# Hybrid diffusion backbone step: the modulation product in four units per tile of the attention with half sums, and the output projection's first weights split in quarters

## The chip, the cores and the metric

The kernel runs on one core of one Trainium2 chip. The metric is the device time of one execution in microseconds: 1143.93 us is the median of three executions of the kernel before, which lay between 1142.75 and 1150.54 us.

## What is computed

One step of a backbone of two layers on 640 tokens of width 1024 (512 latent ones and 128 of context), all in float32. Cut to what matters here, a layer is

```
mod = silu(c) @ w_ada + b_ada                  # 1024 x 6144: shift1, scale1, gate1, shift2, scale2, gate2
h = rms_norm(x, norm1) * (1 + scale1) + shift1
q, k, v, ... = split(h @ w_in)                 # 8 query heads, 2 key heads, width 64
attn = softmax(q k^T) v                        # context rows read context keys, latent rows all 640
merged = concat(rms_norm(attn), rms_norm(sgu), rms_norm(conv))
x = x + gate1 * (merged @ w_out)
h2 = rms_norm(x, norm2) * (1 + scale2) + shift2
x = x + gate2 * hierarchical_moe(h2)           # 16 experts, 2 for each token
```

`mod` is needed for two vectors only (latent `c`, context `c_ctx`). Its first third is due before `h`; the other two thirds (gate1 on) are due after the attention.

## The kernel before, in words

Each engine has its own instruction list, written out by hand, and runs it in order; semaphores join the lists. TensorE (PE) multiplies, ScalarE (ACT) and VectorE (DVE) move results and do the softmax, GpSimd (POOL) does small statistics, the convolution and some transfers, SyncE (SP) issues the loads of the weights.

**Weights.** They come through `raw`, a ring of `RAWS` = 4 buffers of 1 MB, in the fixed order `STREAM`: in a layer eight units of `w_in`, then 16 units of `w_ada` (numbers 8 to 23), then four units of `w_out` (w 8 to 11). SP loads a unit when the one four places ahead has been used (`unit_used`, L355 and L362). A `w` unit is used by splitting it for a product of float32 accuracy: ACT copies it, rounded, to `wH` (`split_hi`, L651, 128x2048), and DVE writes the rest `raw - wH` to `wL` (`split_lo`, L997). An `ada` unit is used by PE straight from `raw` (`ada_mm`, L1407): 4 products of 512 columns in program text, for 128 of the 1024 input rows and 2048 of the columns of `mod`. Eight of them sum up one piece in PSUM bank 7. DVE adds the bias (`piece_add`, L970), and POOL writes the piece to DRAM (`piece_out`) and later loads it back as rows for all partitions.

**Attention.** Five tiles of 128 query rows, first the context tile, whose rows read 128 keys, then four latent ones with 640 keys. Each tile has 8 heads; a head of a tile is a step u, from 0 to 39. Four more values of u finish the last ones. In the step u
- PE makes the scores of u (L1514, L1515), transposes the probabilities of u-2 (L1525), and in an even step multiplies those of a pair of heads with the values (L1540). In an odd step it transposes a pair's result (L1530). In the first two steps of a tile it transposes queries of the next tile (`q_round`, L1493), into bank 7 too, so that a piece has to be read before;
- DVE takes the row maximum of u (L1122), copies transposed probabilities of an even head (L1130), and in an odd step divides a pair (`pair_out`, L1092, L1093). At the third step of a tile it makes the low part of queries (`q_lo`, L1021); at steps 16, 24, 32 and 40 it scales a finished tile (L1099);
- ACT copies transposed probabilities of an odd head (L780), takes the exponential of u (L787), copies a pair's result (L741), and squares finished tiles (L746).

The maximum of u waits for the scores of u; the exponential waits for the maximum; the scores of u+2 wait for the exponential of u, since there are two buffers.

**What stands at which step** is set by two tables. `ADA_AT` gives the number of `ada` units of PE at the end of each step: 0, 0, 1, 1, 1, 1, 2, 2 in the first tile and 0, 0, 2, 2, 1, 1, 1, 1 in the third. `PIECE_AT` follows from it: DVE sums up at the steps 7 and 23. `W_AT` places the splits of w 8 and w 9 on ACT and DVE at the steps 33 and 37, in the last tile. Units w 10 and w 11 are split after the attention.

After the last step PE transposes the merged rows (`merged_chunk`, L1567) and starts the output projection with w 8.

Of the kernel before, what the change touches and what calls it, by code (L numbers as in the profile page):

```python
# [19 lines left out]
NT = 5  # L20
NLT = 4
# [9 lines left out]
N = 512  # L31
# [22 lines left out]
for _l in range(DEPTH):  # L54
# [9 lines left out]
    "ada_read": 24, "piece_done": 3, "piece_out": 2 * 64, "bias_in": 3 * 64,  # L64
    "norm2_row": 16, "a2_row": 2, "params_loaded": 15 * 16, "taps_loaded": 32, "tabs": 6, "modc_psum": 1, "a1_ready": 1,
    "ss1": NT, "rstd1": NT, "xr_ready": NT, "hT_psum": KD, "h_full": 2 * KD, "h_hi": KD, "h_lo": KD,
    "w_hi": 12, "w_lo": 12, "w_used": 6, "proj": 4 * NT, "proj_read": 4 * NT, "zpn_zero": 2,
# [17 lines left out]
def build(nc, I, O):  # L85
    with ExitStack() as ctx:
# [169 lines left out]
        def unit_used(eng, i):  # L256

            kind, l, n = STREAM[i]
            if kind == "ada":
                eng.wait_ge(sem("ada_read"), at("ada_read", l, n + 1))  # L260
            else:
                eng.wait_ge(sem("w_lo"), at("w_lo", l, n + 1))
# [183 lines left out]
        def _(pl):  # L446
# [49 lines left out]
            for l in range(DEPTH):  # L496
# [34 lines left out]

                piece_out(l, 1)
                bias_in(l, 2)
                rest_stats(0)
                attn_stats(0)
# [81 lines left out]
        def _(act):  # L617
# [27 lines left out]
            for l in range(DEPTH):  # L645
                def split_hi(i):
# [4 lines left out]
                    act.activation(wH[:, i % HLS, :], raw[:, POS["w", l, i] % RAWS, :], ACT.Copy).then_inc(sem("w_hi"), 1)  # L651

# [117 lines left out]
                for u in range(NT * NH + 4):  # L770
# [18 lines left out]
                    if u in W_AT:  # L789
                        split_hi(W_AT[u])  # L790
# [150 lines left out]
        def _(dve):  # L941
# [29 lines left out]

            def modc_out(l):
# [21 lines left out]
            for l in range(DEPTH):  # L994
                def split_lo(i):
                    dve.wait_ge(sem("w_hi"), at("w_hi", l, i + 1))
# [118 lines left out]
                for u in range(NT * NH + 4):  # L1115
# [17 lines left out]
                    if u in W_AT:  # L1133
                        split_lo(W_AT[u])
# [9 lines left out]
                    if u in PIECE_AT:  # L1144
                        piece_add(l, 1 + PIECE_AT.index(u))
# [238 lines left out]
        def _(pe):  # L1384
# [37 lines left out]
            for l in range(DEPTH):  # L1422
# [26 lines left out]
                for i in range(8):  # L1449
                    nb, half = divmod(i, 2)  # L1450
                    for k in range(4):
# [3 lines left out]
                        if k == 0:  # L1455
                            pe.wait_ge(sem("w_lo"), at("w_lo", l, i + 1))
# [45 lines left out]
                for u in range(NT * NH + 4):  # L1502
# [90 lines left out]
                for kt in range(KD):  # L1593
                    i, k = 8 + kt // 4, kt % 4
                    pe.wait_ge(sem("mT_lo"), at("mT_lo", l, 2 * kt + 2))
                    if k == 0:
                        pe.wait_ge(sem("w_lo"), at("w_lo", l, i + 1))
# [10 lines left out]
                for t in range(NT):  # L1608
                    if t >= 2:
                        pe.wait_ge(sem("oproj"), at("oproj", l, NT + t - 1))  # L1610
                    for kt in range(KD):
                        i, k = 10 + kt // 4, kt % 4
                        if t == 0 and k == 0:
                            pe.wait_ge(sem("w_lo"), at("w_lo", l, i + 1))
# [146 lines left out]
```

## Time and profile before

| | |
|---|---|
| median of three executions | 1143.93 us |
| the profiled execution's own time | 1141.14 us |
| span of its instructions | 1139.3 us |
| mean granted clock of TensorE | 0.915 |
| busy: PE, DVE, ACT, POOL | 943.4, 673.7, 590.3, 264.5 us |
| PE: idle just before `ada_mm` (L1407) | 33.7 us, of them 33.2 for loads of `w_ada` |

The span lies 1.8 us below the time of its execution. Times of the trace count from the span's start. A busy figure is a mean over stages with different limits, so what matters is which wait ends last in the stage that is changed: the attention, some 116 us of layer 0 and 114 us of layer 1. A row of the timeline gives start, duration, engine, line, operation, and in brackets the idle time before it with what ended it.

### The profile page before, as it was taken

The numbers are of one execution on the slowest core, as the hardware profiler recorded it, in microseconds if no ns is written. First come the engines' busy times: TensorE is split into PE (matmuls) and PEld (weight loads), VectorE is DVE, ScalarE is ACT, GpSimd is POOL, SyncE is SP. The second block draws the span as 40 slices with busy tenths as digits, with TensorE's granted clock in tenths as the row PEclk, the third lists the DMA queues.
The fourth block names the chain that finished last, engine by engine and source line by source line (L and its number), as shares of the span: only waits on it lengthen the run. The fifth ranks groups of instructions, "written<-read, shape, count | busy, mean of one in ns | idle before, by whom it ended". The sixth has DMA issues, their size and how long they took to land.

```text
span 1139.3 us, 14992 instructions
## 1 busy us (share of the span) xinstructions
PE 943.4 (83%) x5232; PEld 737.7 (65%) x5232; DVE 673.7 (59%) x929; ACT 590.3 (52%) x901; POOL 264.5 (23%) x306
## 2 busy tenths in 40 slices
PE   3799988996999499999319999799789949999920
PEld 0488864775778278887218888377568837888710
DVE  0349223565264689989372941365635758998946
ACT  1662233665232288888275332366623408888832
POOL 3024016011041112221250410620202312222133
PEclk9999997998898699999759999899989959999975
DMA  9955227342153989999771240636223358999853
GB/s 323 273 211 209 74 60 305 156 168 86 56 212 112 369 313 399 413 409 366 191 276 47 74 148 10 241 144 267 97 72 130 107 201 303 398 421 417 345 186 128
DMA packets 85951, 248.36 MB, mean 218 GB/s; under 512 B 25644, under 2 KB 30252, under 8 KB 75656
## 3 DMA queue, kind: packets, MB, share of 16 engines
q1 hardware_dynamic: 72760, 209.54, 49.0%
q0 software_dynamic: 11696, 32.86, 8.4%
q10 hardware_dynamic: 1440, 5.24, 1.1%
q8 instruction: 33, 0.54, 0.2%
q14 instruction: 22, 0.18, 0.1%
HBM read 221.07 MB, written 30.21 MB: 221 GB/s over the span
## 4 chain that ended last, share of the span: by engine, by line
PE 65%; DMA 14%; DVE 8%; ACT 7%; issue 4%; POOL 1%; SPq 0%; ACTq 0%; POOLq 0%; DVEq 0%
PE ps L1390 12%; PE ps L1392 11%; PE ps L1391 11%; DMA pool<-in_moe_w 7%; DMA raw<-in_w_ada 4%; PE ps L1540 3%; PE ps L1407 3%; PE ps L1397 3%; PE ps L1399 3%; PE ps L1398 3%; PE ps L1525 3%; DVE wL L1196 2%; ACT wH L841 2%; PE ps L1514 2%; PE ps L1656 2%
## 5 line engine op out<-in xcount | busy, mean ns | idle before, releaser
L1390 PE MATMUL ps<-wH,actH 128*128 128x512 f32 x608 | 247.3, 407 | 7.5 <-DVE actL L1325 5.9
L1392 PE MATMUL ps<-wH,actL 128*128 128x512 f32 x608 | 240.7, 396 | 0.0
L1391 PE MATMUL ps<-wL,actH 128*128 128x512 f32 x608 | 239.8, 394 | 0.0
L1196 DVE TENSOR_TENSOR wL<-raw,wH 128x2048 fp32r<-128x2048 f32 x64 | 146.2, 2285 | 12.2 <-ACT wH L841 12.1
L841 ACT ACTIVATE wH<-raw 128x2048 fp32r<-128x2048 f32 x64 | 122.4, 1912 | 30.7 <-DMA raw<-in_moe_w 27.7
L1390 PEld LDWEIGHTS ps<-wH,actH 128*128 128x128 f32 x608 | 116.5, 192 | 32.9 <-issue 8.5
L1392 PEld LDWEIGHTS ps<-wH,actL 128*128 128x128 f32 x608 | 115.9, 191 | 25.7
L1391 PEld LDWEIGHTS ps<-wL,actH 128*128 128x128 f32 x608 | 116.5, 192 | 22.6
L1397 PE MATMUL ps<-wH,actH 128*128 128x512 f32 x256 | 105.4, 412 | 4.2 <-DVE wL L1196 2.8
L1399 PE MATMUL ps<-wH,actL 128*128 128x512 f32 x256 | 102.2, 399 | 0.0
L1398 PE MATMUL ps<-wL,actH 128*128 128x512 f32 x256 | 101.6, 397 | 0.0
L581 POOL DMA_INDIRECT pool<-h2s,idxc x28 | 52.3, 1867 | 195.7 <-PE ps L1656 156.6
L1122 DVE TENSOR_REDUCE nmax<-ps 128x1 f32<-128x640 f32 (+1 forms) x80 | 57.3, 716 | 63.8 <-PE ps L1515 62.3
L1407 PE MATMUL ps<-raw,cpad 128*32 128x512 f32 x384 | 64.0, 760 | 33.7 <-DMA raw<-in_w_ada 33.2
L1196 DVE TENSOR_TENSOR wL<-pool,wH 128x2048 fp32r<-128x2048 f32 x32 | 73.2, 2287 | 15.8 <-ACT wH L841 15.8
L787 ACT ACTIVATE pool<-ps,nmax 128x640 f32<-128x640 f32 (+1 forms) x80 | 56.5, 706 | 46.4 <-DVE nmax L1122 42.8
L997 DVE TENSOR_TENSOR wL<-raw,wH 128x2048 fp32r<-128x2048 f32 x24 | 54.7, 2291 | 29.0 <-ACT wH L651 28.8
L1525 PE MATMUL ps<-ident,pool 128*128 128x128 f32 x336 | 54.5, 289 | 16.7 <-DVE pool L1130 14.2
L651 ACT ACTIVATE wH<-raw 128x2048 fp32r<-128x2048 f32 x24 | 45.9, 1930 | 38.4 <-PE ps L1392 38.4
L841 ACT ACTIVATE wH<-pool 128x2048 fp32r<-128x2048 f32 x32 | 61.2, 1912 | 5.0 <-DMA pool<-in_moe_w 5.0
L1397 PEld LDWEIGHTS ps<-wH,actH 128*128 128x128 f32 x256 | 49.2, 192 | 15.9 <-DVE wL L1196 3.8
L877 ACT ACTIVATE actH<-ps 128x512 fp32r<-128x512 f32 x64 | 38.3, 598 | 39.3 <-PE ps L1656 36.9
(228 smaller groups left out, 1579.6 us busy)
## 6 DMA issues: line engine op xcount, KB each, us to landing
raw<-in_w_ada SPq DMA_DIRECT2D x48, 1024.0 KB, 7.3
raw<-in_moe_w SPq DMA_DIRECT2D x96, 512.0 KB, 8.4
raw<-in_w_in SPq DMA_DIRECT2D x16, 1024.0 KB, 9.1
raw<-in_moe_w SPq DMA_DIRECT2D x16, 1024.0 KB, 13.1
pool<-in_moe_w SPq DMA_DIRECT2D x32, 512.0 KB, 8.1
pool<-in_moe_w SPq DMA_DIRECT2D x16, 1024.0 KB, 12.9
ys<-pool SPq DMA_DIRECT2D x32, 512.0 KB, 12.1
raw<-in_w_out SPq DMA_DIRECT2D x8, 1024.0 KB, 7.7
```

Of the source, the lines that this page charges most:

```text
L787: act.activation(prob[:, u % 2, 0:keys], flat[:, 2 * N * (u % 2):2 * N * (u % 2) + keys], ACT.Exp, bias=nmax[:, u % 2:u % 2 + 1], accum_ou ...
L841: act.activation(wH[:, i if place is None else place, :], mraw[parity][i], ACT.Copy).then_inc(sem(f"m_hi{i}"), 1)
L1122: dve.tensor_reduce(nmax[:, u % 2:u % 2 + 1], flat[:, 2 * N * (u % 2):2 * N * (u % 2) + keys], X, ALU.max, negate=True).then_inc(sem("nmax ...
L1196: dve.tensor_tensor(wL[:, w, :], mraw[parity][i], f32(wH[:, w, :]), ALU.subtract).then_inc(sem(f"m_lo{i}"), 1)
L1390: pe.matmul(out, aH, wH[:, slot_, cols_], start=first, stop=False)
L1391: pe.matmul(out, aH, wL[:, slot_, cols_], start=False, stop=False)
L1392: return pe.matmul(out, aL, wH[:, slot_, cols_], start=False, stop=last)
L1397: pe.matmul(out, aH, hi, start=first, stop=False)
L1398: pe.matmul(out, aH, lo, start=False, stop=False)
L1399: return pe.matmul(out, aL, hi, start=False, stop=last)
L1407: m = pe.matmul(ps[32 * j:32 * j + 32, ada_bank(l, q), :], c32, raw[:, POS["ada", l, n] % RAWS, j * N:(j + 1) * N], start=(kt == 0), stop= ...
L1525: m = pe.transpose(ps[:, 4 + c // 4, (c % 4) * P:(c % 4) * P + P], prob[:, w % 2, c * P:(c + 1) * P], ident[:, :])
```

## The change

- `ADA_AT` is now 0, 0, 1, 1, 1, 1, 0, 0 in each of the first four tiles: one `ada` unit at the end of the steps 2 to 5, 10 to 13, 18 to 21 and 26 to 29.
- A group of sums in PSUM is now four units, a half of a piece. DVE empties bank 7 at the steps 7, 15, 23 and 31 (`half_add`): the first half is added to the bias, the second half to that sum. PE waits for it before `q_round` at the steps 8, 16 and 24. It is one more reading of the bank for each piece.
- w 8 and w 9 are split in quarters of 512 columns, one in each of the steps 31 to 38, on ACT (`quarter_hi`) and DVE (`quarter_lo`), in the place where the whole split stood in a step. What waited for a split of w 8 or w 9 waits for its fourth quarter.
- On POOL `piece_out(l, 1)` and `bias_in(l, 2)` stand behind `rest_stats(0)` and `attn_stats(0)`, no longer ahead of them.

```diff
-        none, third = (0,) * NH, (0, 0, 2, 2, 1, 1, 1, 1)
-        ADA_AT = (0, 0, 1, 1, 1, 1, 2, 2) + none + third + none + none
-        PIECE_AT = [u for u in range(NT * NH) if ADA_AT[u] and sum(ADA_AT[:u + 1]) % KD == 0]
-        W_AT = {33: 8, 37: 9}
+        ADA_AT = (0, 0, 1, 1, 1, 1, 0, 0) * NLT + (0,) * NH
+        HALF_AT = {8 * t + 7: t for t in range(NLT)}
+        QUARTER_AT = {31 + i: (8 + i // 4, i % 4) for i in range(8)}
...
-                piece_out(l, 1)
-                bias_in(l, 2)
                 rest_stats(0)
                 attn_stats(0)
+                piece_out(l, 1)
+                bias_in(l, 2)
...
+                def quarter_hi(i, j):
+                    if j == 0:
+                        unit_loaded(act, "w", l, i)
+                        w_read(act, l, i - HLS)
+                    act.activation(wH[:, i % HLS, j * N:(j + 1) * N], raw[:, POS["w", l, i] % RAWS, j * N:(j + 1) * N], ACT.Copy
+                                   ).then_inc(sem("quarter_hi"), 1)
...
+            def half_add(l, i):
+                q, half = 1 + i // 2, i % 2
+                dve.wait_ge(sem("ada_read"), at("ada_read", l, KD * q + 4 * half + 4))
+                if half == 0:
+                    dve.wait_ge(sem("bias_in"), at("bias_in", l, 64 * (q + 1)))
+                    dve.tensor_tensor(piece[q], ps[:, ada_bank(l, q), :], bpiece[q], ALU.add).then_inc(sem("piece_half"), 1)
+                else:
+                    dve.wait_ge(sem("piece_half"), at("piece_half", l, q))
+                    dve.tensor_tensor(piece[q], ps[:, ada_bank(l, q), :], piece[q], ALU.add).then_inc(sem("piece_done"), 1)
...
+                def quarter_lo(i, j):
+                    dve.wait_ge(sem("quarter_hi"), at("quarter_hi", l, 4 * (i - 8) + j + 1))
+                    dve.tensor_tensor(wL[:, i % HLS, j * N:(j + 1) * N], raw[:, POS["w", l, i] % RAWS, j * N:(j + 1) * N],
+                                      f32(wH[:, i % HLS, j * N:(j + 1) * N]), ALU.subtract).then_inc(sem("quarter_lo"), 1)
...
-                    if u in W_AT:
-                        split_lo(W_AT[u])
+                    if u in QUARTER_AT:
+                        quarter_lo(*QUARTER_AT[u])
...
-                    if u in PIECE_AT:
-                        piece_add(l, 1 + PIECE_AT.index(u))
+                    if u in HALF_AT:
+                        half_add(l, HALF_AT[u])
...
+                group = 4 if q else KD
...
-                                  start=(kt == 0), stop=(kt == KD - 1))
+                                  start=(kt % group == 0), stop=(kt % group == group - 1))
...
-                                pe.wait_ge(sem("piece_done"), at("piece_done", l, 1 + sum(p_ < u for p_ in PIECE_AT)))
+                                if t % 2:
+                                    pe.wait_ge(sem("piece_half"), at("piece_half", l, (t + 1) // 2))
+                                else:
+                                    pe.wait_ge(sem("piece_done"), at("piece_done", l, 1 + t // 2))
```

The lines of the changed kernel have other numbers: scores L1546 and L1547 (before L1514, L1515), transposes of probabilities L1557 (L1525), of a result L1562 (L1530), values L1572 (L1540), `ada_mm` L1439 (L1407).

PE of the kernel before, the steps 5 (its last row), 6 and 7, and the first scores of step 8:

```order
L1407 MATMUL ps<-raw,cpad 32x512 x4
L1514 MATMUL ps<-actH,actL 128x128
L1515 MATMUL ps<-actH,actL 128x128
L1525 MATMUL ps<-ident,pool 128x128
L1540 MATMUL ps<-tabs,pool 64x128 x2
L1407 MATMUL ps<-raw,cpad 32x512 x8
L1514 MATMUL ps<-actH,actL 128x128
L1515 MATMUL ps<-actH,actL 128x128
L1525 MATMUL ps<-ident,pool 128x128
L1530 MATMUL ps<-ident,pool 128x128
L1407 MATMUL ps<-raw,cpad 32x512 x8
L1514 MATMUL ps<-actH,actL 128x512
```

And in the changed kernel:

```order
L1439 MATMUL ps<-raw,cpad 32x512 x4
L1546 MATMUL ps<-actH,actL 128x128
L1547 MATMUL ps<-actH,actL 128x128
L1557 MATMUL ps<-ident,pool 128x128
L1572 MATMUL ps<-tabs,pool 64x128 x2
L1546 MATMUL ps<-actH,actL 128x128
L1547 MATMUL ps<-actH,actL 128x128
L1557 MATMUL ps<-ident,pool 128x128
L1562 MATMUL ps<-ident,pool 128x128
L1546 MATMUL ps<-actH,actL 128x512
```

The two double units behind the steps 6 and 7 are gone; they stand, one each, behind the steps 10 to 13 now.

DVE in the last tile of the kernel before, from the maximum of step 33 to that of step 36:

```order
L1122 TENSOR_REDUCE nmax<-ps 128x1
L1092 RECIPROCAL rinv<-rsum 128x2
L1093 TENSOR_TENSOR pool<-ps,rinv 128x2x64
L997 TENSOR_TENSOR wL<-raw,wH 128x2048
L1122 TENSOR_REDUCE nmax<-ps 128x1
L1130 COPY pool<-ps 128x640
L1122 TENSOR_REDUCE nmax<-ps 128x1
L1092 RECIPROCAL rinv<-rsum 128x2
L1093 TENSOR_TENSOR pool<-ps,rinv 128x2x64
L1122 TENSOR_REDUCE nmax<-ps 128x1
```

And in the changed kernel, from the maximum of step 33 to the quarter of step 35:

```order
L1153 TENSOR_REDUCE nmax<-ps 128x1
L1123 RECIPROCAL rinv<-rsum 128x2
L1124 TENSOR_TENSOR pool<-ps,rinv 128x2x64
L1028 TENSOR_TENSOR wL<-raw,wH 128x512
L1153 TENSOR_REDUCE nmax<-ps 128x1
L1161 COPY pool<-ps 128x640
L1028 TENSOR_TENSOR wL<-raw,wH 128x512
L1153 TENSOR_REDUCE nmax<-ps 128x1
L1123 RECIPROCAL rinv<-rsum 128x2
L1124 TENSOR_TENSOR pool<-ps,rinv 128x2x64
L1028 TENSOR_TENSOR wL<-raw,wH 128x512
```

The subtraction of 2048 columns behind step 33 has become one of 512 columns in each step, always between the maximum of that step and the maximum of the next.

## Rows read from the trace of the kernel before

**Rows 1.** The page: span, and the chain that ended last, by engine
```profile
span 1139.3 us, 14992 instructions
...
PE 65%; DMA 14%; DVE 8%; ACT 7%; issue 4%; POOL 1%; SPq 0%; ACTq 0%; POOLq 0%; DVEq 0%
```

**Rows 2.** Stretches, layer 0: from:to, length, busy by engine, clock, DMA share, GB/s
```profile
167.47:190.07 22.60, 17.19 (x104) 6.12 (x105) 6.27 (x17) 7.81 (x26) 18.07 (x6) 0.79 0.68 260
190.07:206.97 16.90, 16.60 (x129) 13.51 (x125) 10.94 (x20) 11.50 (x30) 5.63 (x12) 0.88 0.44 172
206.97:232.23 25.26, 25.12 (x232) 16.21 (x230) 13.47 (x27) 14.24 (x35) 1.72 (x5) 1.00 0.62 242
232.23:249.57 17.34, 17.06 (x169) 14.75 (x165) 11.98 (x22) 11.83 (x31) 1.65 (x5) 1.00 0.37 135
249.57:283.96 34.39, 24.68 (x211) 20.17 (x210) 20.46 (x38) 19.07 (x43) 6.82 (x12) 0.90 0.28 93
```

**Rows 3.** Stretches, layer 1, first two tiles
```profile
719.46:740.74 21.28, 16.66 (x104) 5.84 (x104) 6.94 (x17) 6.55 (x25) 18.08 (x6) 0.84 0.68 261
740.74:756.70 15.96, 15.07 (x128) 12.24 (x125) 11.04 (x20) 11.34 (x30) 5.69 (x12) 1.00 0.51 202
```

**Rows 4.** Timeline of PE, end of the first tile of layer 0
```profile
178.72 0.33 PE L1514 MATMUL ps<-actH,actL 128*128 128x128 f32 x1
...
179.60 1.06 PE L1407 MATMUL ps<-raw,cpad 128*32 128x512 f32 x8
...
182.45 1.07 PE L1407 MATMUL ps<-raw,cpad 128*32 128x512 f32 x8 [1.79 <-DMA raw<-in_w_ada]
...
188.21 1.93 PE L1407 MATMUL ps<-raw,cpad 128*32 128x512 f32 x8 [1.33 <-DMA raw<-in_w_ada]
```

**Rows 5.** Timeline of DVE, last tile of layer 0
```profile
249.17 0.82 DVE L1122 TENSOR_REDUCE nmax<-ps 128x1 f32<-128x640 f32 x1 [1.26 <-PE ps L1515]
...
252.11 1.00 DVE L1099 TENSOR_SCALAR pool<-pool,stat 128x256 f32<-128x256 f32 x3
...
253.45 0.83 DVE L1122 TENSOR_REDUCE nmax<-ps 128x1 f32<-128x640 f32 x1 [0.35 <-PE ps L1515]
...
257.33 2.29 DVE L997 TENSOR_TENSOR wL<-raw,wH 128x2048 fp32r<-128x2048 f32 x1 [2.65 <-ACT wH L651]
...
259.54 0.82 DVE L1122 TENSOR_REDUCE nmax<-ps 128x1 f32<-128x640 f32 x1
...
274.64 0.82 DVE L1122 TENSOR_REDUCE nmax<-ps 128x1 f32<-128x640 f32 x1
```

**Rows 6.** Timeline of ACT, last tile of layer 0
```profile
254.62 0.79 ACT L787 ACTIVATE pool<-ps,nmax 128x640 f32<-128x640 f32 x1
...
255.39 1.91 ACT L651 ACTIVATE wH<-raw 128x2048 fp32r<-128x2048 f32 x1
...
260.39 0.79 ACT L787 ACTIVATE pool<-ps,nmax 128x640 f32<-128x640 f32 x1 [3.10 <-DVE nmax L1122]
```

**Rows 7.** Timeline of PE, last tile of layer 0
```profile
261.23 0.74 PE L1525 MATMUL ps<-ident,pool 128*128 128x128 f32 x5 [3.54 <-DVE pool L1130]
...
276.50 1.30 PE L1525 MATMUL ps<-ident,pool 128*128 128x128 f32 x5 [0.42 <-ACT pool L780]
...
277.73 2.14 PE L1540 MATMUL ps<-pool 128*64 128x128 f32 x20
...
281.36 1.31 PE L1540 MATMUL ps<-tabs,pool 128*64 128x128 f32 x20 [0.68 <-ACT tabs L780]
```

**Rows 8.** Timeline of DVE, two subtractions of 512 columns
```profile
167.88 0.69 DVE L1021 TENSOR_TENSOR actL<-pool,actL 128x512 fp32r<-128x512 f32 x1 [2.88 <-ACT actL L674]
...
172.92 1.93 DVE L1021 TENSOR_TENSOR actL<-pool,actL 128x512 fp32r<-128x512 f32 x1 [0.81 <-ACT actL L674]
```

**Rows 9.** Timeline of ACT, a copy of 512 columns
```profile
167.22 0.62 ACT L674 ACTIVATE actL<-pool 128x512 fp32r<-128x512 f32 x1
```

**Rows 10.** Timeline of POOL, the last of six convolution steps
```profile
183.65 2.89 POOL L516 TENSOR_TENSOR pool<-pool 128x1280 f32<-128x1280 f32 x1
```

More of the change, by code:

```diff
@@ L63 @@
 PER_LAYER = {
-    "ada_read": 24, "piece_done": 3, "piece_out": 2 * 64, "bias_in": 3 * 64,
+    "ada_read": 24, "piece_half": 2, "piece_done": 3, "piece_out": 2 * 64, "bias_in": 3 * 64,
     "norm2_row": 16, "a2_row": 2, "params_loaded": 15 * 16, "taps_loaded": 32, "tabs": 6, "modc_psum": 1, "a1_ready": 1,
     "ss1": NT, "rstd1": NT, "xr_ready": NT, "hT_psum": KD, "h_full": 2 * KD, "h_hi": KD, "h_lo": KD,
-    "w_hi": 12, "w_lo": 12, "w_used": 6, "proj": 4 * NT, "proj_read": 4 * NT, "zpn_zero": 2,
+    "w_hi": 10, "w_lo": 10, "quarter_hi": 8, "quarter_lo": 8, "w_used": 6, "proj": 4 * NT, "proj_read": 4 * NT, "zpn_zero": 2,
     "sq": 2 * NT, "ssqk": 2 * NT, "rqk": 2 * NT, "kv_raw": NT, "sv_raw": NT, "q_final": NT, "k_final": NT,
@@ L261, in unit_used, with w_split @@
             else:
-                eng.wait_ge(sem("w_lo"), at("w_lo", l, n + 1))
+                w_split(eng, l, n)
+        def w_split(eng, l, n):
+            if n in (8, 9):
+                eng.wait_ge(sem("quarter_lo"), at("quarter_lo", l, 4 * (n - 7)))
+            else:
+                eng.wait_ge(sem("w_lo"), at("w_lo", l, n + 1 if n < 8 else n - 1))
         def unit_loaded(eng, kind, l, n):
@@ L530, in rest_stats @@
                     pl.tensor_tensor(stat[:, c + 16:c + 18], stat[:, c:c + 2], nhalf[:, 0:2], ALU.pow).then_inc(sem("rstd3b"), 1)
+                rest_stats(0)
+                attn_stats(0)
                 piece_out(l, 1)
                 bias_in(l, 2)
-                rest_stats(0)
-                attn_stats(0)
                 rest_stats(1)
@@ L995, in split_lo @@
                 def split_lo(i):
-                    dve.wait_ge(sem("w_hi"), at("w_hi", l, i + 1))
+                    dve.wait_ge(sem("w_hi"), at("w_hi", l, i + 1 if i < 8 else i - 1))
                     dve.tensor_tensor(wL[:, i % HLS, :], raw[:, POS["w", l, i] % RAWS, :], f32(wH[:, i % HLS, :]),
                                       ALU.subtract).then_inc(sem("w_lo"), 1)
+                def quarter_lo(i, j):
+                    dve.wait_ge(sem("quarter_hi"), at("quarter_hi", l, 4 * (i - 8) + j + 1))
+                    dve.tensor_tensor(wL[:, i % HLS, j * N:(j + 1) * N], raw[:, POS["w", l, i] % RAWS, j * N:(j + 1) * N],
+                                      f32(wH[:, i % HLS, j * N:(j + 1) * N]), ALU.subtract).then_inc(sem("quarter_lo"), 1)
                 split_lo(0)
@@ L1132, in _ @@
                         pair_out((u - 5) // 2)
-                    if u in W_AT:
-                        split_lo(W_AT[u])
+                    if u in QUARTER_AT:
+                        quarter_lo(*QUARTER_AT[u])
                     if u >= 16 and u % 8 == 0:
@@ L1455, in _ @@
                         if k == 0:
-                            pe.wait_ge(sem("w_lo"), at("w_lo", l, i + 1))
+                            w_split(pe, l, i)
                         for t in range(NT):
@@ L1547, in _ @@
                             if h == 0 and t:
-                                pe.wait_ge(sem("piece_done"), at("piece_done", l, 1 + sum(p_ < u for p_ in PIECE_AT)))
+                                if t % 2:
+                                    pe.wait_ge(sem("piece_half"), at("piece_half", l, (t + 1) // 2))
+                                else:
+                                    pe.wait_ge(sem("piece_done"), at("piece_done", l, 1 + t // 2))
                             q_round(t + 1, h)
@@ L1596, in _ @@
                     if k == 0:
-                        pe.wait_ge(sem("w_lo"), at("w_lo", l, i + 1))
+                        w_split(pe, l, i)
                     for t in range(NT):
```

4 lines of the change are left out of this document (2 added, 2 removed).

## The prediction

> **What bounds the kernel now.** I read the page first, for its chain of waits: PE holds 65% of it, so what the attention costs is what PE does or waits for in it [rows 1]. Then I cut the attention at the first scores of each tile. Layer 0 has 22.60, 16.90, 25.26, 17.34 and 34.39 us for its five tiles, the last one up to the first transpose of merged rows [rows 2]; layer 1 has 21.28 and 15.96 us for the first two [rows 3] and the same as layer 0, within 0.2 us, for the rest. The reader is to see four different limits:
> - The fourth tile has no ada unit, and PE is busy for 17.06 of 17.34 us. The third has eight, and PE is busy for 25.12 of 25.26 [rows 2]. PE is the bound in both, and an ada unit costs (25.26 - 17.34) / 8 = 0.99 us there.
> - The first tile is bound by loads. PE is busy for 17.19 of 22.60 us, DMA for 0.68, and the clock is at 0.79 [rows 2]. The timeline of PE shows that the first four units went without a wait (they were in the ring already); the second unit of step 6 waited 1.79 us for its load and the last one of step 7 1.33 us, and that last one took 1.93 us, where one at the upper clock takes 1.07 [rows 4]: PE had idled, and the clock had dropped from 2.4 to 1.2 GHz.
> - The second tile begins at the lower clock in layer 0 (0.88 in its stretch) [rows 2]; without that, layer 1 needs 15.96 us for it [rows 3].
> - The last tile should need about what the fourth does. Here PE idles 3.54 us once for each split, behind DVE [rows 7]. The chain: exponential of step 33 on ACT at 254.62, the split's copy 255.39 for 1.91 us [rows 6], then DVE's subtraction at 257.33 for 2.29 us, and only then the maximum of step 34, at 259.54 [rows 5]. From 253.45 that is 6.09 us in which DVE starts no other maximum.
>
> **First part: the ada units, step by step.** The sum is made against the profiled execution.
> First tile. The steps up to 5 don't change. The scores of step 6 start at 178.72 and its own work is over at 179.60, where the ada units follow [rows 4]: 0.88 us. Step 7 has the same kinds of work and one transpose more, I take 1.0. So step 8 starts at 180.5 and not at 190.07: 9.6 us gained in layer 0. With the same 13.1 us in layer 1 it is 21.28 - 13.1 = 8.2 us. Four of the eight units in this are only moved; the rest is the waits for loads and the low clock.
> Second tile. It gets four units: 4 x 0.99 = 4.0 us over the 15.96 us that it has at the upper clock [rows 3], 19.9 us, against 16.90 and 15.96: a loss of 3.0 and 4.0 us. Some of it may go into idle time (PE has 0.9 us of it in layer 1's second tile), which I leave out. The loads of these four units are issued as before, when the buffers of the first four come free, in the steps 2 to 5. The last of them was there at 188.21 [rows 4] and is now wanted at step 13, some 12 us after 180.5: covered. If this cover were gone, the wait would be at most the 1.79 + 1.33 us and one between them again.
> Third tile: four units fewer, 4.0 us gained. Fourth: four more, 4.0 us lost. That pair gives nothing.
> Up to step 32 this is 9.6 - 3.0 = 6.6 us in layer 0 and 8.2 - 4.0 = 4.2 us in layer 1, together 10.8 us.
>
> **The half sums** are two more readings of 512 columns in a layer, and each is an addition as long as a q_lo, 0.69 us [rows 8]. At the steps 7, 15 and 23 they stand behind pair_out, for which PE's product with the values waits anyway, and at 15 and 23 that product, 1.31 us [rows 7], covers them: nothing. At step 7 the product is a short one of the context tile, so PE may wait for 0.3 us. The maximum of the next step comes 0.6 us late and has the other steps' slack. The one at step 31 is on the path and stands in the sum below. On POOL the moved piece_out and its bias are wanted at step 23 and later, 20 us after step 15; the statistics that now stand ahead of them come earlier. SP gets w 8's buffer at step 26 and no longer 20, four steps with an ada unit and more ahead of step 31, about 14 us; nothing else is moved past a queue.
> One queue is met anew. The convolution on POOL ends with a step from 183.65 to 186.54 [rows 10], and q_lo of step 10 falls near it now (before, it came after). In the conv the same operation took 1.93 us and not 0.69 [rows 8]. That is at most 1.24 us of DVE. I take nothing, because PE has an ada unit in each of those steps to work on, and keep 1.2 us a layer for the range. The Trainium skill (SBUF — State Buffer, "Who interferes with whom") says that a DVE instruction with two SBUF inputs contends with a GpSimd instruction that reads SBUF, as q_lo and these steps do. The row agrees, and by the rule 1.2 us a layer would be lost if nothing hid it; the half sums read PSUM and would be free.
>
> **Second part: the quarters.** No row shows a step with a quarter, so I rebuild one from rows. From a maximum to its exponential 0.85 us (259.54 to 260.39), from there to the next ACT instruction 0.77 (254.62 to 255.39) [rows 5, 6], the copy of 512 columns 0.62 [rows 9], 0.03 until DVE starts (255.39 + 1.91 to 257.33), and 0.61 until the next maximum (the subtraction takes 0.69 [rows 8], and the maximum at 259.54 starts 0.08 before the end of 257.33 + 2.29 [rows 5]). The sum is 2.88 us a step, one after the other, since each quarter waits for the exponential of its own step. The steps of the fourth tile take 17.34 / 8 = 2.17 us. So eight quarters are not hidden: they make the steps 31 to 38 last 23.0 us, with 0.6 for the half sum at 31 and 0.9 for the scaling at step 32 (1.00 us for three) [rows 5], 24.5 us. Before, the maxima of the steps 31 and 39 lie at 249.17 and 274.64: 25.5 us. The same stall, in eight pieces: 1.0 us gained.
> What comes behind gains a little more. From the maximum of 39 to the transposes of 38 there are 1.86 us now (274.64 to 276.50), with ACT late; they, and the product behind them, run at half the clock, 1.30 and 2.14 us where 0.74 and 1.31 are full speed [rows 7]. With no idle time of 3.5 us on PE the clock should stay up: 1.4 us. The squares that ACT has behind the quarters of the steps 36 and 38 come off that again, some 0.4. I take 2.0 us a layer, with bounds of 3.5 (ACT is in time too) and -3.5 (the clock, below).
>
> **Sum.** 10.8 + 2 x 2.0 = 14.8 us. The profiled execution took 1141.14 us, the median is 2.8 us above it: 1143.9 - 14.8 = 1129.1, say 1129 us.
>
> **Rivals.**
> (a) The clock falls in the last tile. PE has gaps in every step there, 2.88 - 2.17 = 0.7 us each. For it: in the first tile of layer 0 short work with gaps between went with 0.79 [rows 2]. Against it: PE is busy for three quarters of the time. The price: a pair of steps lasts 4.28 us at full clock (249.17 to 253.45 [rows 5]) and about 1.7 times as much at half (2.14 / 1.31), 7.3 us, more than the 5.7 of two quarters. Four pairs and the tail make 5.5 us a layer over my forecast: 1129 + 11 = 1140 us. The Trainium skill (TensorE: Matmul & The Clock Gate, "A second HAM failure mode: psum-queue depth-cycling") tells of such a case, where PE idles for short times between groups of matmuls and the clock swings; by that it would be this rival.
> (b) The loads aren't hidden: with units in four tiles the ring runs empty in the second tile, or w 8 is late at step 31. It returns about 3.8 us a layer at most, 1137 us. Against it are the 12 and 14 us above.
> (c) Slower: the quarter puts three engines in series. If the scores of the next step came only after it, PE's transposes, 0.74 us [rows 7], and the scores, about as long again (an estimate from there), would join the 2.88 and make 4.3 us a step, 34 us for eight and not 25.5, a loss of 9 us a layer: 1144 - 10.8 + 18 = 1151 us. It decides from 3.9 us a step on. Against it: scores of u+1 wait for the exponential of u-1 only, which is there one step earlier, and the split of 6.09 us cost PE 3.54 us, not all of it.
> (d) The quarters are hidden better than I think and the last tile falls to what the fourth takes plus little: 5 us more in each layer, 1119 us. Against it the fixed order on DVE.
>
> **How the numbers follow.** Forecast with its neighbourhood 0.68, (a) 0.16, (b) 0.08, (c) 0.04, (d) 0.04. The forecast's own bounds are 1129 - 3 (tail in time) - 1 and 1129 + 2.4 (q_lo) + 3: 1125 to 1134. The range reaches on to (a) on one side and half way to (d) on the other: 1121 to 1140. Within 1% of 1143.9, about what a measurement of this kernel can tell from no change, begins at 1132.5; nearly all of the forecast and (d) lie below, some of (b) too: 0.70 faster, 0.26 the same, 0.04 slower.
>
> **What would show it right or wrong.** In the changed kernel: no wait of ada_mm for w_ada in the attention; tiles of 13, 20, 21.3 and 21.3 us; in both layers maxima every 2.9 us in the steps 31 to 38, and PE's largest idle time there below 1.5 us; the granted clock near 1.0 from the first tile's end to the last tile. Steps of 3.9 us or more, a clock of 0.5 to 0.8 in the last tile, or waits for w_out would prove me wrong.

## The result and the profile after

The changed kernel needs 1126.44 us (median of four executions, 1123.17 to 1129.09). The kernel before needed 1144.14 us in the comparison (median of four). The ratio is 0.984 with a 95% interval of 0.981 to 0.987, so 14.5 to 21.5 us are gained. The profiled execution of the changed kernel took 1123.17 us, of the kernel before 1141.14 us: 18.0 us less, and the span is 18.0 us shorter too.

The page of the changed kernel: the span, the chain that ended last by engine, and the group of `ada_mm`, which answer to [rows 1] and to the table of the front.

```profile
span 1121.3 us, 15024 instructions
...
PE 68%; DMA 10%; DVE 10%; ACT 7%; issue 4%; POOL 1%; SPq 0%; ACTq 0%; POOLq 0%; DVEq 0%
...
L1439 PE MATMUL ps<-raw,cpad 128*32 128x512 f32 x384 | 62.8, 739 | 25.7 <-DMA raw<-in_w_ada 25.2
```

The share of DMA in the chain has fallen from 14% to 10%. Idle time ahead of `ada_mm` was 33.7 us and is 25.7 us, all but 0.5 of it for loads; what is left lies outside the attention. The share of DVE has risen from 8% to 10%: that fits the last tile, where DVE and ACT now wait for each other in each step (below).

The stretches of the changed kernel, cut as in [rows 2] and [rows 3]: the five tiles of layer 0, then the first two of layer 1 (from:to, length, busy time of PE, its weight loads, DVE, ACT and POOL, granted clock, DMA share, GB/s).

```profile
168.37:182.86 14.49, 12.62 (x73) 5.57 (x73) 6.32 (x15) 7.28 (x24) 13.64 (x5) 0.76 0.53 191
182.86:202.50 19.64, 18.73 (x158) 12.75 (x158) 11.36 (x23) 11.68 (x33) 5.94 (x6) 1.00 0.78 284
202.50:223.84 21.34, 21.20 (x199) 15.36 (x198) 13.10 (x26) 13.23 (x33) 5.85 (x13) 1.00 0.58 212
223.84:245.21 21.37, 21.23 (x199) 15.36 (x198) 12.39 (x25) 12.83 (x32) 1.65 (x5) 1.00 0.53 190
245.21:277.20 31.99, 23.68 (x212) 18.75 (x210) 21.27 (x45) 19.56 (x49) 5.95 (x13) 0.95 0.32 109
...
708.78:721.42 12.64, 11.21 (x72) 5.39 (x73) 5.99 (x15) 6.09 (x23) 11.79 (x4) 0.86 0.45 152
721.42:741.06 19.64, 18.73 (x157) 12.75 (x158) 11.36 (x23) 11.68 (x33) 7.73 (x7) 1.00 0.86 329
```

The reader is to see four tiles in which PE is busy for all but 2 us or less, and a last one in which it idles for 8.3 of 31.99 us. The five tiles take 108.83 us (before 116.49), in layer 1 107.15 us (before 114.10): 14.6 us of the 18.0. The other 3.4 us lie where the change has moved no instruction: up to the first scores -0.9, between the two attentions 3.9 (431.6 us and not 435.5), behind the second 0.4.

PE in the first tile, to be read against [rows 4] (start, duration, engine, line, operation, in brackets the idle time before it and what ended it):

```profile
172.40 1.94 PE L1439 MATMUL ps<-raw,cpad 128*32 128x512 f32 x8 [0.38 <-ACT actL L748]
...
175.12 1.94 PE L1439 MATMUL ps<-raw,cpad 128*32 128x512 f32 x8
...
180.28 1.07 PE L1439 MATMUL ps<-raw,cpad 128*32 128x512 f32 x8
...
181.27 0.33 PE L1546 MATMUL ps<-actH,actL 128*128 128x128 f32 x1
...
182.15 0.33 PE L1546 MATMUL ps<-actH,actL 128*128 128x128 f32 x1
...
182.86 0.47 PE L1546 MATMUL ps<-actH,actL 128*128 128x512 f32 x1
```

Steps 6 and 7 take 0.88 and 0.71 us, and no unit waits for a load. The first two units took 1.94 us each, so PE was at the lower of its two clock levels, 1.2 GHz, for them.

DVE in the last tile, to be read against [rows 5]:

```profile
254.72 0.69 DVE L1028 TENSOR_TENSOR wL<-raw,wH 128x512 fp32r<-128x512 f32 x1 [1.07 <-ACT wH L665]
255.33 0.82 DVE L1153 TENSOR_REDUCE nmax<-ps 128x1 f32<-128x640 f32 x1
256.06 0.81 DVE L1161 COPY pool<-ps 128x640 f32<-128x640 f32 x1
257.62 0.69 DVE L1028 TENSOR_TENSOR wL<-raw,wH 128x512 fp32r<-128x512 f32 x1 [0.74 <-ACT wH L665]
258.23 0.82 DVE L1153 TENSOR_REDUCE nmax<-ps 128x1 f32<-128x640 f32 x1
...
269.91 0.81 DVE L1153 TENSOR_REDUCE nmax<-ps 128x1 f32<-128x640 f32 x1
```

ACT beside it, to be read against [rows 6]:

```profile
256.18 0.79 ACT L802 ACTIVATE pool<-ps,nmax 128x640 f32<-128x640 f32 x1 [1.49 <-DVE nmax L1153]
...
256.96 0.62 ACT L665 ACTIVATE wH<-raw 128x512 fp32r<-128x512 f32 x1
```

Read together: maximum at 255.33, exponential at 256.18, copy of the quarter at 256.96, its subtraction at 257.62, next maximum at 258.23. One after the other, 2.90 us a step; DVE waits for ACT (1.07, 0.74 us) and ACT for DVE (1.49 us) in the same step.

PE in the same tile, to be read against [rows 7]:

```profile
262.82 0.74 PE L1557 MATMUL ps<-ident,pool 128*128 128x128 f32 x5 [1.09 <-DVE tabs L1161]
...
265.98 1.29 PE L1557 MATMUL ps<-ident,pool 128*128 128x128 f32 x5
...
267.20 1.53 PE L1572 MATMUL ps<-tabs,pool 128*64 128x128 f32 x20
```

Idle times of 1.0 to 1.3 us stand where 3.54 us stood once for each split, and there is one short piece at the lower clock.

### The profile page after: what moved, and what is told of

Its sections match the earlier page's. It is cut to its first block, busy times and chain, and to the rows that moved or that the text cites. A ratio compares the mean times of both kernels' runs of the same rounds, so it can differ in the third digit from the quotient of the medians.

```text
span 1121.3 us, 15024 instructions
## 1 busy us (share of the span) xinstructions
PE 937.7 (84%) x5232; PEld 733.4 (65%) x5232; DVE 674.9 (60%) x945; ACT 591.5 (53%) x913; POOL 260.7 (23%) x306
## 4 chain that ended last, share of the span: by engine, by line
PE 68%; DMA 10%; DVE 10%; ACT 7%; issue 4%; POOL 1%; SPq 0%; ACTq 0%; POOLq 0%; DVEq 0%
PE ps L1421 12%; PE ps L1423 12%; PE ps L1422 12%; DMA pool<-in_moe_w 5%; PE ps L1439 4%; PE ps L1428 4%; PE ps L1430 4%; PE ps L1429 4%; PE ps L1557 3%; PE ps L1572 3%; PE ps L1546 2%; PE ps L1692 2%; ACT wH L856 2%; DVE wL L1227 2%; PE ps L1547 2%
## 5 line engine op out<-in xcount | busy, mean ns | idle before, releaser
L1227 DVE TENSOR_TENSOR wL<-raw,wH 128x2048 fp32r<-128x2048 f32 x64 | 146.0, 2283 | 11.6 <-ACT wH L856 11.4
L856 ACT ACTIVATE wH<-raw 128x2048 fp32r<-128x2048 f32 x64 | 122.4, 1912 | 28.7 <-DMA raw<-in_moe_w 25.5
L1439 PE MATMUL ps<-raw,cpad 128*32 128x512 f32 x384 | 62.8, 739 | 25.7 <-DMA raw<-in_w_ada 25.2
L1557 PE MATMUL ps<-ident,pool 128*128 128x128 f32 x336 | 53.3, 284 | 9.1 <-DVE tabs L1161 4.7
L659 ACT ACTIVATE wH<-raw 128x2048 fp32r<-128x2048 f32 x20 | 38.3, 1935 | 38.4 <-PE ps L1423 38.4
L1023 DVE TENSOR_TENSOR wL<-raw,wH 128x2048 fp32r<-128x2048 f32 x20 | 45.5, 2290 | 18.5 <-ACT wH L659 18.3
```

Of the source, the lines that this page charges most:

```text
L856: act.activation(wH[:, i if place is None else place, :], mraw[parity][i], ACT.Copy).then_inc(sem(f"m_hi{i}"), 1)
L1227: dve.tensor_tensor(wL[:, w, :], mraw[parity][i], f32(wH[:, w, :]), ALU.subtract).then_inc(sem(f"m_lo{i}"), 1)
L1557: m = pe.transpose(ps[:, 4 + c // 4, (c % 4) * P:(c % 4) * P + P], prob[:, w % 2, c * P:(c + 1) * P], ident[:, :])
```

## The experiments

Each ratio is to executions of the kernel before that ran beside the kernel in question on the same chip; their medians were 1144.14 us for the changed kernel, 1145.75 us for the next four rows of the table, 1142.72 us for "no unit in the first tile", "quarters of two columns" and "POOL in the old order". So the ratios are to be compared, not the medians. The stretches come from one profile of each kernel; "attention" is the sum of the ten stretches of both layers (before 230.59 us, changed kernel 215.98 us).

| kernel | median us | ratio, 95% interval | attention | last tile, layers 0 and 1 |
|---|---|---|---|---|
| changed | 1126.44 | 0.984, 0.981 to 0.987 | 215.98 | 31.99, 32.15 |
| units alone | 1132.05 | 0.992, 0.988 to 0.995 | 222.06 | 35.45, 35.03 |
| quarters alone | 1136.33 | 0.992, 0.989 to 0.995 | 223.03 | 31.14, 31.15 |
| quarters a step later | 1114.18 | 0.973, 0.969 to 0.977 | 204.13 | 25.07, 25.07 |
| whole splits a step later | 1116.32 | 0.975, 0.972 to 0.978 | 205.93 | 26.77, 26.77 |
| no unit in the first tile | 1138.51 | 0.996, 0.994 to 0.999 | 225.82 | 35.62, 35.25 |
| quarters of two columns | 1118.06 | 0.976, 0.971 to 0.981 | 205.37 | 25.69, 25.69 |
| POOL in the old order | 1135.07 | 0.993, 0.991 to 0.995 | 224.61 | 31.77, 32.19 |

### Units and half sums alone

The changed kernel with w 8 and w 9 split whole at the steps 33 and 37, as before.

```diff
-        QUARTER_AT = {31 + i: (8 + i // 4, i % 4) for i in range(8)}
+        QUARTER_AT = {33: 8, 37: 9}
...
-                    act.activation(wH[:, i % HLS, j * N:(j + 1) * N], raw[:, POS["w", l, i] % RAWS, j * N:(j + 1) * N], ACT.Copy
-                                   ).then_inc(sem("quarter_hi"), 1)
+                    act.activation(wH[:, i % HLS, :], raw[:, POS["w", l, i] % RAWS, :], ACT.Copy).then_inc(sem("quarter_hi"), 1)
```

> The units in four tiles with half sums, w 8 and w 9 split whole at the steps 33 and 37 as before. Theory (the two parts add up, each in its own tiles): the first four tiles take what they take in the changed kernel (76.8 and 75.0 us in the two layers, 10.1 us less than before), the last tile 34.3 us in each as before, so about 10 us less than before, a ratio of 0.991. Rival 1 (the 3.4 us that the span gained outside of the attention belong to this part): 0.988. Rival 2 (the parts need one another): the gain of tiles 0 to 3 shows in the stretches but comes back as waits in the last tile, 0.995 or more.

Measured: 0.992. The first four tiles take 76.64 and 74.94 us (before 82.10 and 79.84, changed kernel 76.84 and 75.00). The last one is 1.1 and 0.8 us longer than before, where no difference was expected. Its stretch in layer 0:

```profile
244.25:279.70 35.45, 25.77 (x211) 20.86 (x210) 20.86 (x39) 18.98 (x43) 7.20 (x13) 0.86 0.29 97
```

What follows: the first part gives its 10.4 us up to step 32 by itself, and 1.8 us are lost in the last tile. The attention nets 8.5 us. The half sum of step 31 is not what costs them: the steps 31 and 32 take 1.74 and 2.54 us here and took 1.32 and 2.96 before, 4.28 us both times, and the kernel of "No unit in the first tile" has no sum there and a last tile just as long (35.62 and 35.25 us). In layer 0 the difference lies behind step 39, from whose maximum to the first transpose of merged rows it takes 10.50 us where it took 9.32. PE there:

```profile
271.33 1.30 PE L1555 MATMUL ps<-ident,pool 128*128 128x128 f32 x5 [0.55 <-ACT pool L793]
...
274.89 1.33 PE L1555 MATMUL ps<-ident,pool 128*128 128x128 f32 x5
```

Both groups of transposes are at the lower clock; before, only the first one was [rows 7], and the second took 0.77 us. In layer 1 the difference lies between the maxima of 31 and 39, 26.18 us apart and not 25.38, with a granted clock of 0.85 in the tile and not 0.90. Why the clock is lower, no run shows.

### Quarters alone

Tables, sums and POOL's order as before, the quarters of the change.

```diff
-        ADA_AT = (0, 0, 1, 1, 1, 1, 0, 0) * NLT + (0,) * NH
-        HALF_AT = {8 * t + 7: t for t in range(NLT)}
+        none, third = (0,) * NH, (0, 0, 2, 2, 1, 1, 1, 1)
+        ADA_AT = (0, 0, 1, 1, 1, 1, 2, 2) + none + third + none + none
+        PIECE_AT = [u for u in range(NT * NH) if ADA_AT[u] and sum(ADA_AT[:u + 1]) % KD == 0]
```

> The units, the whole sums and POOL's order as before, w 8 and w 9 in quarters. Theory: only the last tile changes, from 34.3 to 32.1 us in each layer, about 4.5 us less than before, a ratio of 0.996. Rival 1 (the 3.4 us outside of the attention belong to the quarters, since w 8 and the loads behind it come at other times): 0.993. Rival 2 (the quarters bring nothing by themselves): 1.000.

Measured: 0.992, with an interval that ends below the 0.996 of the expectation and holds the 0.993 of its first rival. That rival put the rest outside of the attention, and the traces don't: of 8.5 us of the span 7.6 lie in it, 6.4 in the two last tiles and 1.2 in the first four tiles of both layers together. The last tile, 3.2 and 3.1 us shorter than before:

```profile
249.26:280.40 31.14, 22.46 (x211) 17.66 (x209) 20.68 (x44) 19.55 (x49) 5.66 (x12) 1.00 0.33 103
```

The maxima of the steps 31 and 39 are 24.49 us apart (25.47 before, 25.10 in the changed kernel, which has the half sum between them). What follows: the quarters gain 6.4 us over both last tiles, and of that only 1 us a layer is the stall itself. The rest is behind step 39, where PE comes at full clock and ACT in time. In the last tiles the two parts happen to add up, -6.4 + 1.8 = -4.6 us against -4.5 in the changed kernel, but not for one reason: in the changed kernel 1.2 of the 1.8 us are the half sum of step 31, which does lengthen a step that has a quarter (3.81 us, here 3.21). In the first four tiles this kernel came out 1.2 us shorter than before without an edit there; two executions differ by that much and more (the first tile in "No unit in the first tile").

### Quarters, DVE's part one step later

One line differs from the changed kernel: DVE subtracts the quarter of step u behind the maximum of step u+1, where ACT's copy has been there for a step.

```diff
-                    if u in QUARTER_AT:
-                        quarter_lo(*QUARTER_AT[u])
+                    if u - 1 in QUARTER_AT:
+                        quarter_lo(*QUARTER_AT[u - 1])
```

> The changed kernel, but each quarter's subtraction on DVE stands one step behind its copy on ACT. Theory (the 2.88 us of a step are a chain, since DVE waits in each step for the exponential and the copy of the same step): with the wait gone DVE has some 3.9 us of work in a pair of steps and ACT 3.4, less than PE's 4.28, so PE is the bound again, a pair takes 4.3 to 4.5 us instead of 5.8, and the last tile 26 to 27 us instead of 32: 10 to 11 us less than the changed kernel, 0.975 of the kernel before. Rival (DVE's work itself, or the order of its instructions, is the bound): 31 us or more for the last tile, 0.984.

Measured: 0.973, the lowest ratio of all, with the expected 0.975 inside its interval. The last tile of layer 0:

```profile
244.69:269.76 25.07, 21.54 (x211) 17.43 (x209) 20.86 (x45) 19.23 (x49) 6.50 (x13) 1.00 0.42 140
```

DVE in it:

```profile
254.00 0.68 DVE L1028 TENSOR_TENSOR wL<-raw,wH 128x512 fp32r<-128x512 f32 x1
254.60 0.82 DVE L1153 TENSOR_REDUCE nmax<-ps 128x1 f32<-128x640 f32 x1
...
256.06 0.68 DVE L1028 TENSOR_TENSOR wL<-raw,wH 128x512 fp32r<-128x512 f32 x1
257.14 0.82 DVE L1153 TENSOR_REDUCE nmax<-ps 128x1 f32<-128x640 f32 x1 [0.40 <-PE ps L1547]
```

No subtraction waits for ACT. DVE does the same work as in the changed kernel (20.86 against 21.27 us busy) in 6.9 us less. The maxima of 31 and 39 are 17.35 us apart, 2.17 a step: just what the fourth tile took before. What follows: the 2.9 us a step of the changed kernel are not work, but the series of exponential, copy and subtraction within one step. The two last tiles are 14.0 us shorter than in the changed kernel; the whole attention is 11.9 us shorter, since the first tile of layer 1, the same in both, took 14.99 us here and 12.64 there.

### Whole splits, DVE's part one step later

The kernel with the units alone, with the same one-line edit for the whole subtraction, now at the steps 34 and 38.

```diff
-                    if u in QUARTER_AT:
-                        quarter_lo(QUARTER_AT[u])
+                    if u - 1 in QUARTER_AT:
+                        quarter_lo(QUARTER_AT[u - 1])
```

> As e1_units (whole splits, copies at the steps 33 and 37), but DVE subtracts one step later, at 34 and 38. Theory (what counts is that DVE doesn't wait for a copy of its own step, not the size of the pieces): exponential and maximum come up to 1.6 us late in two steps, which the two score buffers hide (about 1.8 us of slack), and the last tile takes 27 to 29 us, 0.977 to 0.980 of the kernel before, better than the changed kernel. Rival (the size counts; a piece of 2048 columns always stalls PE): 32 us or more for the last tile, 0.985 or more.

Measured: 0.975, somewhat better than the 0.977 to 0.980 expected. DVE, around the first split of layer 0:

```profile
253.81 2.29 DVE L1026 TENSOR_TENSOR wL<-raw,wH 128x2048 fp32r<-128x2048 f32 x1 [0.87 <-ACT wH L664]
256.02 0.82 DVE L1151 TENSOR_REDUCE nmax<-ps 128x1 f32<-128x640 f32 x1
```

The wait ahead of it is 0.87 us where it was 2.65 [rows 5]. The steps with a split take 4.78 and 4.61 us, and from 31 to 39 it is 20.01 us, 2.7 more than with late quarters. What follows: the late subtraction alone takes the two last tiles from 70.48 us (units alone) to 53.54, 16.9 us; quarters with it take them to 50.14, another 3.4 us off. Most hangs on the order on DVE, and less on the size of the pieces. In the whole attention only 1.8 of these 3.4 us show, since the first tiles, which are the same in both, took 14.29 and 14.99 us with the late quarters and 15.06 and 12.62 here; the intervals of the two ratios overlap.

### Quarters of two columns

The changed kernel, but each quarter copies and subtracts only the first 2 of its 512 columns. It leaves out nearly all of the split of w 8 and w 9, and keeps each wait.

```diff
-                    act.activation(wH[:, i % HLS, j * N:(j + 1) * N], raw[:, POS["w", l, i] % RAWS, j * N:(j + 1) * N], ACT.Copy
+                    act.activation(wH[:, i % HLS, j * N:j * N + 2], raw[:, POS["w", l, i] % RAWS, j * N:j * N + 2], ACT.Copy
```

> The changed kernel, but each of the eight quarters copies and subtracts only its first 2 of 512 columns: most of the split of w 8 and w 9 is left out. Theory (the step is the chain maximum, exponential, copy, subtraction): without the length of the two splits, 0.62 and 0.69 us, the chain shrinks to some 2.1 to 2.2 us a step, no more than PE's own 2.17, and the last tile takes 25 to 27 us, like e3_lag with its 25.07. Rival (the instructions and their waits cost, whatever their size): 28 us or more.

Measured: 0.976. DVE:

```profile
253.90 0.16 DVE L1028 TENSOR_TENSOR wL<-raw,wH 128x2 fp32r<-128x2 f32 x1 [0.31 <-ACT wH L665]
253.97 0.82 DVE L1153 TENSOR_REDUCE nmax<-ps 128x1 f32<-128x640 f32 x1
```

The subtraction still waits for ACT, and the last tile falls to 25.69 us. The two last tiles take 51.38 us where the changed kernel has 64.14, so the width of 16 quarters with their copies costs 12.8 us there, 0.80 us each. (Over the whole attention the difference is 10.6 us, because the first tile of layer 1 took 14.95 us here and 12.64 there.) What follows: the full width has this price only in series with the exponential of its own step. A step later it is hidden, and a last tile with it takes 25.07 us. The wait without the width costs little too.

### No unit in the first tile

Whole splits as in the kernel with the units alone, eight units in the second tile and eight in the third, with whole sums.

```diff
-        ADA_AT = (0, 0, 1, 1, 1, 1, 0, 0) * NLT + (0,) * NH
+        none, third = (0,) * NH, (0, 0, 2, 2, 1, 1, 1, 1)
+        ADA_AT = none + third + third + none + none
```

> As e1_units (whole splits at 33 and 37, POOL's changed order), but no ada unit in the first tile and eight in each of the second and third, at the steps 10 to 15 and 18 to 23 in the pattern 2, 2, 1, 1, 1, 1, with whole sums: no half sums at all. Theory (the gain of the first part is that no unit is asked for before its load is there; the half sums only make four tiles possible): the first tile takes 9 to 11 us, bound by the steps' own waits, the second 15.96 + 8 x 0.99 = 23.9, the third 25.3, the fourth 17.3, together 76 to 78 us a layer as in e1_units (76.6 and 74.9), the last tile 34.3 instead of 35.2: the same time as e1_units within 3 us, ratio 0.991. Rival (eight units in one tile drain the ring wherever they stand, since four buffers hold four units): waits for loads of 3 to 4 us in the second tile, 0.996 or more.

Measured: 0.996, where 0.991 was expected, and in the traces 3.8 us more in the attention than with four units in each tile (the intervals of the two ratios, 0.988 to 0.995 and 0.994 to 0.999, just overlap). The 0.996 is the figure of the rival, but not for its reason: PE waits for no load, in the stretches of the first and second tile:

```profile
168.19:179.53 11.34, 9.05 (x40) 6.98 (x41) 5.21 (x15) 7.35 (x23) 10.52 (x4) 0.52 0.02 6
179.53:203.34 23.81, 23.72 (x190) 14.43 (x188) 11.82 (x24) 12.95 (x35) 9.24 (x7) 0.94 0.65 265
```

The second tile starts at the lower clock after a first one at 0.52. The first tile without units takes 11.34 us in both layers, with four it takes 14.28 in layer 0 and 12.58 in layer 1 (units alone). That is 0.7 and 0.3 us for a unit, where one costs 0.99 us in a tile that PE bounds. The price isn't fixed. The six kernels with four units in the first tile took 12.6 us for it at a granted clock of 0.86, 14.3 to 14.5 us at 0.76 and 15.0 to 15.2 us at 0.66, so a unit costs from 0.3 to nearly 1 us there, and which of the three comes up differs between kernels whose instructions up to that point are the same. What follows: in the first tile PE has room that nothing else fills, more or less of it by its clock. Waits for loads are gone with eight units in the second tile as well, so those of before hung on the place of the units of the steps 6 and 7, close behind the first four, and not on their number in a tile. The half sums are worth something because they leave four units in the first tile. They are not what makes the last tile longer: there is none here, and it takes 35.62 and 35.25 us.

### POOL in the old order

The changed kernel with the transfers of piece and bias ahead of the statistics, as before.

```diff
-                rest_stats(0)
-                attn_stats(0)
                 piece_out(l, 1)
                 bias_in(l, 2)
+                rest_stats(0)
+                attn_stats(0)
```

> The changed kernel with POOL's order as before: piece_out and bias_in ahead of the statistics of the first tile. Theory (POOL is in order; piece_out now waits for the sum of step 15, and the two cost 2.06 + 2.02 us of issue, so that rstd3b, for which DVE waits at step 16, comes some 5 us late): DVE stalls at step 16 for about 4 to 5 us less 1.8 of slack, the third tile takes 24 to 25 us instead of 21.3, 5 to 7 us in both layers, 0.989 to 0.991 of the kernel before. Rival (no DVE instruction behind it is wanted soon): the third tile stays at 21.3, the time that of the changed kernel.

Measured: 0.993, in the traces 8.6 us more in the attention than the changed kernel. The third tile takes 26.17 and 24.69 us where it took 21.34 and 21.35, 8.2 us over both layers, more than the 5 to 7 expected. In layer 0 the granted clock of that tile was 0.93, in layer 1 it was 1.00. POOL in it:

```profile
204.90 2.06 POOL L495 DMA_DIRECT2D modrow<-misc  x4 [17.45 <-DVE misc L996]
206.97 2.02 POOL L488 DMA_DIRECT2D pool<-in_b_ada  x4
...
209.33 0.70 POOL L538 TENSOR_TENSOR stat<-stat,nhalf 128x2 f32<-128x2 f32 x1
```

And DVE:

```profile
210.07 0.62 DVE L1130 TENSOR_SCALAR pool<-pool,stat 128x256 f32<-128x256 f32 x2 [4.00 <-POOL stat L538]
```

What follows: the second half sum is there only at 204.6 us, POOL waits 17.45 us for it in its order, then issues transfers for 4.1 us, and only then makes the statistics for which the scaling on DVE at step 16 waits. The swap of two pairs of lines saves the change more than half of its gain in the attention.

## Why the prediction was right

The forecast was 1129 us, the median is 1126.4. By its own steps:

- **First tile.** It said 13.1 us in both layers; it was 14.49 and 12.64. The part that the change makes was right: the waits for the second unit of step 6 and the last one of step 7 are gone, and the steps 6 and 7 take 0.88 and 0.71 us (0.88 and 1.0 were forecast). The 1.4 us too many in layer 0 come from "the steps up to 5 don't change": the same instructions took 12.90 us up to step 6 (168.37 to 181.27) where the execution before took 11.25 (167.47 to 178.72), since the clock rose later: two units and part of a third were at the lower one (1.94, 1.94 and 1.27 us), and not one. In layer 1 the error has the other sign. That the two partly offset each other is luck: over the kernels with these four units the tile took 12.6 to 15.2 us.
- **Second to fourth tile.** It said 19.9, 21.3 and 21.3 us; it was 19.64, 21.34 and 21.37 us. The price of 0.99 us for a unit holds where PE is the bound. Up to step 32 the gain was 5.26 and 4.84 us, together 10.1, and 10.8 was forecast.
- **Half sums.** At step 7 the sum cost PE nothing: it lies from 183.53 to 184.21, and PE starts the next tile's queries at 184.26, right behind its product (183.79 and 0.44 us). The 0.3 us allowed for it didn't come. The one at step 31 cost 0.6 us on the path, as in the sum: 0.61 us between the distances of the maxima with and without it (25.10 and 24.49).
- **The queue met anew** wasn't met. The convolution ended at 187.46 us and `q_lo` of step 10 came at 190.29 us and took 0.69 us (layer 1: 727.90 and 728.86). The forecast had the convolution's end at 186.54, from the execution before, and step 10 near it; its zero was right and its reason only half so, for nothing had to hide it. Its "at most 1.24 us" was misread: q_lo of the first tile ends 0.55 us after a step of the convolution each time (the last section), so what it loses is the rest of that step. It took 2.68 us in layer 1 of the kernel before.
- **POOL's order** stood in the forecast at nothing, and that is right for the swap as it is made. What the swap averts, 8.6 us, the forecast had not worked out.
- **A step with a quarter** was put at 2.88 us from six rows and takes 2.90 (255.33 to 258.23). The maxima from 31 to 39 were put at 24.5 us and are 25.10 and 25.09 us apart. Of the missing 0.6 us, half is at step 31, which took 3.81 us (244.81 to 248.62) where 2.88 + 0.6 was forecast; it took 3.21 with the quarters alone, so the half sum has its size and the quarter there is dearer. The step with the scaling took 3.81 us too, and 2.88 + 0.9 was forecast.
- **The last tile** was to gain 2.0 us a layer and gained 2.40 and 2.11 us. The sum is right because two errors offset each other, and that is luck. The forecast had 1.0 us from the stall and 1.0 us behind step 39. The stall gave 0.37 and 0.29 us. Behind step 39 it was 2.03 and 1.81 us: from the maximum to the first transpose of merged rows it takes 7.29 us (269.91 to 277.20) where it took 9.32. In layer 0 the clock's part is as forecast: from the transposes of step 38 to those of merged rows it is 6.18 us (271.02 to 277.20) and was 7.46, 1.3 us less where 1.4 was in the sum. The term for ACT was mis-sized: its squares were to cost 0.4 us, but the transposes of step 38 come 1.11 us after the maximum and not 1.86, 0.75 us gained.
- **Rival (a)**, the clock in the last tile, shows up in one place: transposes of 1.29 us and a product of 1.53 us behind 265.98, and the stretch at 0.95. It costs little, because PE has slack at the step (the maxima stay 2.9 us apart): the same tile at a clock of 1.00 took 31.77 us (POOL in the old order, layer 0), here 31.99. The Trainium skill (TensorE: Matmul & The Clock Gate, "A second HAM failure mode: psum-queue depth-cycling") says that short idle times between groups of matmuls can let the clock swing. This trace shows one swing in 32 us; that the short idle times caused it is not shown. **Rival (b)**, loads: none waits in the attention. **Rival (c)** decides from 3.9 us a step on, and no step reached it; the nearest were the steps 31 and 32 with 3.81 us. **Rival (d)**, the last tile near the fourth's, was refused with "the fixed order on DVE", and that is what the late quarters show: with another order there the last tile is 25.07 us.

Of the signs that the prediction named, no wait for `w_ada` in the attention, the lengths of the second to fourth tile, 2.9 us a step from step 33 on and no idle time of PE above 1.5 us came as written; the clock was 1.00 up to the fourth tile and 0.95 in the last.

So 14.6 us of the attention stand against 14.8 in the forecast. The other 3.4 us of the profiled execution lie mainly between the attentions. That stretch takes 435.5 us in the one profile of the kernel before and 430.3 to 434.2 us in the eight others, the kernel with the quarters alone among them (433.2), in all of which its instructions are the same, though loads of weights may be issued at other times. It scatters by some 4 us without an edit, but that the kernel before has the highest of nine could be chance or not; with one profile of it this stays open.

## What to carry to other kernels

When two engines share the steps of a pipeline and one prepares something for the other, take the result one step later than it is made: here one line took 12 us off (1.1% by the ratios), and did more than the cutting into pieces. A step's price is read from the series of starts across engines, not from busy times. And a moved wait is to be followed on every in-order engine: with POOL's transfers ahead of its statistics, a half sum that is ready later costs more than half of the gain.

## What the runs showed of the hardware that was not expected

- The same matmul work has a price that hangs on what is around it: a unit of `w_ada` costs 0.3 us to nearly 1 us in the first tile and 0.99 us in the others. Without any unit the first tile took 11.34 us, with a granted clock of 0.52 in layer 0 and 0.64 in layer 1. With four units it took 12.6 us at 0.86 (changed kernel, layer 1), 14.49 at 0.76 (changed kernel, layer 0) and 15.18 at 0.66 (POOL in the old order, layer 0).
- PE busy for 74% of the last tile (23.68 of 31.99 us), in short pieces with gaps of 1.0 to 1.3 us, stood with a granted clock of 0.95, and with the quarters alone (72%) it was 1.00. With the splits whole (units alone, 73%) it was 0.86, and before, with gaps of 3.54 us, 0.90 [rows 2, 7].
- A DVE operation with two SBUF inputs waits for the end of a step of the convolution on POOL that runs beside it. In the changed kernel `q_lo` took 2.50 us during such a step, and 0.69 us once the convolution was over. Both lines are DVE's:

```profile
173.26 2.50 DVE L1052 TENSOR_TENSOR actL<-pool,actL 128x512 fp32r<-128x512 f32 x1 [0.84 <-ACT actL L689]
...
190.29 0.69 DVE L1052 TENSOR_TENSOR actL<-pool,actL 128x512 fp32r<-128x512 f32 x1 [0.74 <-ACT actL L689]
```

The step of the convolution beside the first, and the last one, on POOL:

```profile
172.31 2.90 POOL L520 TENSOR_TENSOR pool<-pool,misc 128x1280 f32<-128x1280 f32 x1
...
184.55 2.91 POOL L524 TENSOR_TENSOR pool<-pool 128x1280 f32<-128x1280 f32 x1
```

`q_lo` ends at 175.76, 0.55 us after the step's end at 175.21. In the kernel before it is 0.55 us too: 174.85 [rows 8], after a step from 171.40 to 174.30. So it isn't a factor (3.6 here, 2.8 there) but the rest of the step. The Trainium skill (SBUF — State Buffer, "Who interferes with whom") says that a DVE instruction with two SBUF inputs contends with a GpSimd instruction that reads SBUF. The trace agrees. The half sum of step 7, which reads PSUM and SBUF, took 0.68 us beside a step of the convolution (183.53, on POOL 181.57 to 184.47), as much as without one.
